# One layer of a hybrid diffusion backbone: a unit's second convolution part and the z halves issued ahead of the turning of the probabilities

## The reference

```
qa, ka, va, qb, kb, vb, zb, a_f, a_b, b_f, b_b, ga, gb = split(h @ w_in)
# branch A, 8 heads of 64:
s = q.k * scale (+ learned bias, window of a 2-D band of 256 keys, and 128 cached context keys)
p = softmax(s);  o_a = p @ v
# branch B, the 12 column blocks of qb, kb, vb:
qkv = silu(short_conv(concatenate([qb, kb, vb]), conv_w))      # 5 taps along the tokens
... gated delta rule on qkv, both directions ...
o_b = rms_norm(o_b) * silu(zb)
```

## Time and profile before

| what | value |
|---|---|
| median of 3 runs | 1290.6 us (1290.14 to 1292.92) |
| profiled execution, its own time | 1286.11 us |
| its span | 1284.3 us |
| PE busy | 1144.1 us, 89% of the span |
| DVE, ACT, POOL busy | 445.2, 329.5, 180.2 us |
| granted PE clock, mean over the span | 0.957 |

### The profile page before, as it was taken

The page is one execution under the profiler, slowest core; times in us unless marked ns, Lnnn a source line. Parts: engine busy times, 40 slices in busy tenths (PEclk is TensorE's granted clock), DMA queues, the critical chain, the costliest instruction groups (busy, mean ns, idle before and its releaser), DMA issues.

```text
span 1284.3 us, 15885 instructions
## 1 busy us (share of the span) xinstructions
PE 1144.1 (89%) x6262; PEld 611.6 (48%) x6262; DVE 445.2 (35%) x843; ACT 329.5 (26%) x587; POOL 180.2 (14%) x295
## 2 busy tenths in 40 slices
PE   2699999999998987889999999999649999999990
PEld 1244456666664666888444444444333333333320
DVE  1223035877764542555420300214431111111115
ACT  4012134454453533332321000111202111111111
POOL 0000020011000257571100000000110111111100
PEclk9799999999989999899999999999959999999995
DMA  8801243343302110210231111150616999999936
GB/s 325 360 9 66 90 141 114 132 148 141 122 1 77 47 29 22 87 26 1 94 131 66 51 35 46 66 196 33 245 43 241 385 392 377 375 391 380 385 112 249
DMA packets 44063, 199.98 MB, mean 156 GB/s; under 512 B 18320, under 2 KB 23904, under 8 KB 31952
## 3 DMA queue, kind: packets, MB, share of 16 engines
q1 hardware_dynamic: 28256, 142.03, 28.8%
q10 hardware_dynamic: 4608, 30.18, 6.2%
q0 software_dynamic: 11120, 26.70, 5.8%
HBM read 190.69 MB, written 22.87 MB: 166 GB/s over the span
## 4 chain that ended last, share of the span: by engine, by line
PE 76%; DVE 9%; DMA 6%; POOL 3%; issue 3%; ACT 3%; SPq 0%; DVEq 0%; POOLq 0%; ACTq 0%
PE bank L1649 24%; PE bank L2195 11%; PE bank L1753 8%; PE bank L2216 6%; DMA arena<-h_scratch,arena 3%; PE bank L2052 3%; PE bank L2050 3%; PE bank L1802 2%; PE bank L2183 2%; PE bank L1739 2%; PE bank L1607 2%; PE bank L1908 1%; PE bank L1710 1%; DMA arena<-in_w_blocks 1%; DVE arena L1287 1%
## 5 line engine op out<-in xcount | busy, mean ns | idle before, releaser
L1649 PE MATMUL bank<-arena 128*128 128x512 f32 x720 | 315.9, 595 | 4.4 <-DVE arena L1113 3.5
L1649 PEld LDWEIGHTS bank<-arena 128*128 128x128 f32 x720 | 135.3, 190 | 169.4 <-issue 168.3
L2195 PE MATMUL bank<-arena 128*32 128x512 f32 x1536 | 172.2, 599 | 1.3 <-DVE arena L1562 1.3
L1753 PE MATMUL bank<-arena 128*128 128x320 f32 x384 | 122.0, 452 | 0.5 <-ACT arena L822 0.5
L2195 PEld LDWEIGHTS bank<-arena 128*32 128x32 f32 x1536 | 48.2, 110 | 107.8 <-issue 107.8
L2216 PE MATMUL bank<-arena 128*32 128x512 f32 x768 | 87.4, 595 | 0.8 <-ACT arena L1053 0.8
L1753 PEld LDWEIGHTS bank<-arena 128*128 128x128 f32 x384 | 68.6, 194 | 26.4 <-issue 2.1
L1575 DVE TENSOR_TENSOR arena<-arena,bank 128x256 f32<-128x256 f32 x24 | 10.1, 421 | 175.6 <-ACT arena L1047 175.6
L710 POOL DMA_INDIRECT y_scratch<-arena x24 | 24.3, 1013 | 247.8 <-DVE arena L1568 219.7
L1440 DVE TENSOR_TENSOR arena<-arena,bank 128x512 f32<-128x512 f32 x10 | 6.9, 689 | 135.8 <-PE bank L2052 135.8
L976 ACT ACTIVATE arena<-bank 128x512 f32<-128x512 f32 x20 | 11.9, 597 | 151.5 <-PE bank L1649 151.4
(11 more groups left out here) (298 smaller groups left out, 1517.4 us busy)
## 6 DMA issues: line engine op xcount, KB each, us to landing
arena<-in_w_up SPq DMA_DIRECT2D x32, 2048.0 KB, 10.1
arena<-in_w_blocks SPq DMA_DIRECT2D x27, 2048.0 KB, 7.9
arena<-in_w_down ACTq DMA_DIRECT2D x28, 1024.0 KB, 8.6
arena<-y_scratch SPq DMA_DIRECT2D x10, 512.0 KB, 7.5
arena<-in_bias POOLq DMA_DIRECT2D x3, 1536.0 KB, 11.6
arena<-in_w_down SPq DMA_DIRECT2D x4, 1024.0 KB, 8.0
arena<-in_x SPq DMA_DIRECT2D x5, 512.0 KB, 9.1
gram_scratch<-arena SPq DMA_DIRECT2D x10, 256.0 KB, 2.4
```

The lines of the kernel that those rows point to most:

```text
L1649: last = mm(bank, hT[:, k, tok0[i]:tok0[i] + P], w[:, k, :], start=(k == 0), stop=(k == KC - 1))
L1753: last = mm(banks[5 + half][:, 0:HTOK], w[:, k, :], hT[:, k, half * HTOK:(half + 1) * HTOK], start=(k == 0), stop=(k == KC - 1))
L2195: last = mm(banks[2 + e % 2][at, :], rowsT[e % 2][:, k, at], eup[expert % SLOTS_W][:, k, :], start=(k == 0), stop=(k == KC - 1))
```

## The change

In each iteration the second part of the convolution products (and of the z products in units 37 and 38) is issued before `prob_turn(u)` and no longer behind it. Nothing is added or removed, and the lists of the other engines are as before.

```diff
@@ -1820,11 +1820,11 @@
                     conv_mm(c, 2 * phase)
                 if u in (37, 38):
                     z_mm(u - 37, 0)
-                prob_turn(u)
                 if 0 <= c < 12:
                     conv_mm(c, 2 * phase + 1)
                 if u in (37, 38):
                     z_mm(u - 37, 1)
+                prob_turn(u)
                 if u >= 1:
                     values(u - 1)
                 if u % 4 == 3 and u < 32:
```

## The result

The changed kernel takes 1316.54 us (median of 5 runs, 1304.07 to 1320.56) against 1290.6 us for the kernel before (median of 5 runs, 1284.11 to 1292.92): the ratio is 1.0186, 95% interval 1.0156 to 1.0216. It is slower, by 26 us between the medians and by 18.0 us between the two profiled executions (1286.11 and 1304.07). Run a second time with the experiments, on another chip, it came to 1315.11 us, ratio 1.0189 (1.0160 to 1.0218).

What follows compares the result with a forecast made beforehand. PE, busy 89% of the span, was taken as the bound; 9.2 us of L1761 waits, 0 for shapes and 6.8 us of clock falls made 16.0 us on the 1290.6 median: 1306.6 us, range 1296 to 1317 us.

Steps and rivals of the forecast that it cites:

- No wait to win at L1720: Scaled probabilities keep PE waiting only in unit 0, 1.8 us, which the change does not touch; no gain from turning later.
- The chain and its price: In units 3c + 7, later transposes delay ACT's copy, table load and SiLU, so L1761 waits longer: 9.2 us in all.
- The Trainium skill's drain behind a table load: About 1380 ns behind a table switch on ACT; would lengthen the chain 1.38 us; the forecast went by the trace instead.
- The price of the shapes: Dearer transposes ahead of values against one change of shape spared, 38 units: taken as 0, bounds -4.2 to +3.8 us.
- the row of L1764: Four transposes, then another shape, take 0.53 us before; from it three transposes ahead of values were put at 0.42 to 0.43.
- What else hangs on the transposes: conv_in(c, 0) on ACT, score scaling and weight-slot release wait for nothing new or just fit: 0.
- The clock: New PE gaps at L1761 bring falls to 1.2 GHz, about 3.4 us each: 6.8 us taken, ends 0 and 17.
- two of five gaps: Of five new PE gaps of 1.91 us, two were assumed to bring a clock fall: 2 x 3.4 = 6.8 us.
- My five gaps: PE gaps at L1761 forecast as new, 1.91 us each, at units 10, 16, 22, 28 and 37.
- theory C: Experiments' theory: loss beyond the waits is PE's clock; filling the changed kernel's gaps should give 1296 to 1300 us.
- The rest as before: The stage from 166 to 414 us should grow 9 to 26 us, all other stages unchanged.
- four or five falls: Rival: PE's clock falls at four or five of the new gaps, 1313.4 to 1316.8 us; chance 0.12.

Runs made afterwards that it cites:

- the kernel with the later barrier: Kernel before plus a wait for tok_ready and two identity products on PE between the last values and the barrier: 1295.23 us, ratio 1.0030.

## Why the prediction was right, and where its size was off

*No wait to win at L1720: right.* It waits 1.8 us at unit 0 in both kernels.

*The chain and its price: right.* The distances from the values to L1761 were forecast as 2.79 us and came out 2.79 to 2.80 in every unit but 7 (forecast 2.49, measured 2.63) and 34 (no change forecast, 2.91 against 2.92). Against before that is 0.41 at unit 7, 3 x 1.30, 0.88 and 0.89, 2 x 0.13, 1.04, -0.01 and 1.99, together 9.4 us where I had 9.2. That the chain is the cause is shown from both ends: the order in the units 3c + 7 alone gives the whole loss, in all others none, and taking the SiLU from behind the copy, or the table loads out of the chain, ends it with PE's order unchanged. The Trainium skill's drain behind a table load (ScalarE: Activation LUTs, "What ACT_TABLE_LOAD costs") shows in no run: the SiLU starts 0.01 us behind the load here too, and in this stage of all fourteen profiles ACT's next instruction starts 0.01 to 0.02 us behind each load.

*The price of the shapes: right.* Transposes ahead of values take 0.42 us, as by the row of L1764, and one long piece of products 3.34 instead of 3.43. The sum is 0 to 0.01 us a unit, and the kernel with the order in 27 harmless units can't be told from the one before.

*What else hangs on the transposes: right.* The first convolution product of a chunk waits nowhere in the changed kernel.

*The clock: this term was mis-sized.* I took two of five gaps, 6.8 us. Measured are 13 to 18 us more lost to the clock than before, of them about 10 in this stage. The stretches behind the eight gaps of L1761 in the changed kernel (units 10, 13, 16, 22, 25, 28, 34, 37; the eighth column is the clock):

```profile
227.77:234.26 6.49, 6.49 (x21) 4.45 (x22) 4.38 (x9) 1.99 (x3) 0.00 (x0) 0.74 0.01 3
249.09:256.00 6.91, 6.91 (x17) 4.69 (x18) 3.41 (x6) 1.88 (x3) 0.00 (x0) 0.52 0.03 9
272.06:278.60 6.54, 6.54 (x22) 4.47 (x23) 4.26 (x10) 1.99 (x3) 2.30 (x5) 0.74 0.28 73
311.45:318.00 6.55, 6.55 (x36) 4.54 (x40) 4.73 (x10) 2.48 (x4) 0.00 (x0) 1.00 0.01 3
331.14:338.00 6.86, 6.86 (x17) 4.71 (x18) 3.40 (x6) 1.71 (x2) 0.00 (x0) 0.51 1.01 329
354.10:360.60 6.50, 6.50 (x22) 4.48 (x23) 4.16 (x9) 1.99 (x3) 0.00 (x0) 0.74 0.00 0
393.49:400.00 6.51, 6.51 (x32) 4.75 (x33) 3.47 (x8) 2.48 (x4) 0.00 (x0) 1.00 0.01 3
420.54:427.00 6.46, 6.46 (x21) 3.45 (x22) 3.34 (x7) 1.99 (x3) 0.00 (x0) 1.00 0.00 0
```

By each length times one less its clock, five of the eight had a fall: 1.7, 3.3, 1.7, 3.4 and 1.7 us, together 11.8. The wait of 2.73 us ahead of the z products, which both kernels have, was followed by a fall in both, and it cost 1.7 us more than before (0.47 x 7.20 = 3.4 us against 0.34 x 5.00 = 1.7). The fall at unit 34, 3.4 us, is gone. That makes 10.1 us for the stage. My five gaps were also not all new: those at units 10, 16, 22 and 28 had been there with 0.62 to 0.89 us, and grew. I had the number of falls as a matter of the gap's length, with the border between 1.80 and 2.04 us. Both sides of that are wrong. The gaps of 1.92 at units 22 and 37 and the one of 2.04 at unit 34, behind which the clock had fallen before, did nothing; the gaps of 0.94 at units 13 and 25, which my list of five did not contain, brought the two longest falls. What these have ahead of them is `mod_cols`, eight matmuls of 2 columns, and then the idle time: from 247.10 to 249.09 PE moved next to nothing, though half of that is called busy. With all gaps filled, the falls behind them are gone and the stage is 12.7 us shorter (260.10 to 247.39) though its chain on ACT is the same: that shows that the gaps bring the falls (theory C). With these two alone filled, the falls right behind them are gone as well, but others got longer or came anew, the one behind the gap at unit 34 (2.10 us there) among them, and the stage is 0.75 us shorter. So a fall does not belong to its gap alone; what comes ahead of it in the execution matters too. That `mod_cols` makes its gap worse was argued and not shown. In three profiles with the new order in the units 3c + 7 the falls came each time at the same places in this stage, units 10, 13, 16, 25, 28 and the z products.

*The rest as before: right in the first profile, wrong in the second.* The prediction put nothing behind the barrier. The second profile of the changed kernel took 1314.05 us, 27.9 more than the profile before: 18.0 of them in this stage, 7.4 in the delta rule, the rest further on. That first profile was the fastest of the ten runs of this kernel, so comparing it with the profile before hides this part. The delta rule took 206.5 us in the second profile and 206.4 in that of the units 3c + 7, against 199.1 before and 198.6 in the first profile after. The traces show one place where it grows. Each group below has two operations of DVE, two of POOL, and the matmuls that wait for DVE's next result; first the kernel before, then the changed kernel in its second profile (one line number higher):

```profile
463.24 1.42 DVE L1320 TENSOR_TENSOR arena<-arena 128x512 f32<-128x512 f32 x2
464.10 3.04 POOL L611 TENSOR_TENSOR arena<-arena 128x512 f32<-128x512 f32 x2
465.44 1.38 PE L1899 MATMUL bank<-arena 128*128 128x128 f32 x8 [1.02 <-DVE arena L1296]
```

```profile
481.96 3.42 DVE L1321 TENSOR_TENSOR arena<-arena 128x512 f32<-128x512 f32 x2
481.89 2.95 POOL L612 TENSOR_TENSOR arena<-arena 128x512 f32<-128x512 f32 x2
486.17 1.38 PE L1900 MATMUL bank<-arena 128*128 128x128 f32 x8 [3.03 <-DVE arena L1297]
```

Before, DVE was first; here POOL was first by 0.07 us, DVE's two operations took 2.00 us longer, PE waited 2.01 us longer, and its clock then fell (487.5 to 491.6 us at a mean of 0.58) where it had stayed at 1.00 before (469.0 to 474.0 us). In all fourteen profiles the length of the delta rule goes with this row: 198.6 to 199.4 us in the eight where DVE's pair takes 1.42 us, 201.5 where it takes 2.37 (the kernel with the later barrier), 203.3 in the three with 2.96 to 2.98, 206.4 and 206.5 with 3.39 and 3.42. This is a correlation and was not tested by a run, and what decides which engine comes first stays open.

*The range*, 1296 to 1317, held the median of 1316.54 by half a microsecond, and that was partly luck: the forecast added 16 us and the measured difference is 26; the upper end was worked out from five falls at the gaps of my list, and what filled it was 10 us of clock at other places and a part behind the barrier that the prediction put at nothing. The rival "four or five falls" was nearest in time, 1313 to 1317 us, and it was wrong about where they are.

## What to carry to other kernels

Before moving a piece of work behind another on one engine, follow its signal into the other engines' lists and add up what stands behind the instruction that waits for it: here a copy held up a table load and a SiLU, 2.6 us from the copy to the matmul of the first engine that waited for them. The cheap remedy was at the waiting end: put the activation that needs nothing from PE ahead of the copy that does (1286.4 us instead of 1290.6, and 30 us against the changed kernel). Count each new gap on PE twice, once as a wait and once for the clock (here 9.4 us of waits came with 13 to 18 us of clock). Do not price a fall by the length of its gap: in one execution gaps of 0.94 us had falls behind them and a gap of 2.04 us had none, and filling the short ones brought the fall back at the long one. Take a second profile before you say that the later stages are unchanged.

## What the runs showed of the hardware that I had not expected

Useless matmuls made a kernel faster. Fourteen added products of 512 columns, 14 us of busy PE time in the profile, placed in idle time, took the changed kernel from 1316 to 1300 us. Two of them alone (2.2 us) took 9.5 us off the median, though only 0.75 us off the stage in the profile.

A gap of 0.94 us behind eight matmuls of 2 columns was followed by about 7 us at 1.2 GHz, a gap of 2.04 us behind convolution products and values by none, in the same execution. With the two short gaps filled, the long one (2.10 us there) was followed by 6.8 us at 1.2 GHz.

The same instructions behind the barrier took 198.6 and 206.5 us in two profiles of one kernel: 4.0 us more busy time of PE, with more time at the lower clock, and 3.9 us more idle time. Two operations of DVE on 128x512 elements took 1.42 us when they began ahead of two such operations of POOL, and 3.42 us when POOL began 0.07 us ahead of them.
